# DeltaNet's 16 x 16 diagonal blocks: inverted by matrix products on TensorE, or by recursive doubling on VectorE behind a trip through DRAM

## Time and profile before

| | us |
|---|---|
| median of 3 runs | 1150.86 (1150.45 to 1152.09) |
| the profiled execution | 1150.29 |
| its span, as the profile shows it | 1148.4 |
| TensorE busy | 1133.1 |
| VectorE busy | 707.2 |
| ScalarE busy | 548.3 |
| GpSimd busy | 0.9 |

### The profile page before, as it was taken

One profiled execution on the slowest core, in us unless ns is written; L12 is line 12 of the kernel. 1 busy time (PEld: TensorE's weight loads), 2 busy tenths in 40 slices (PEclk: granted clock), 3 DMA queues, 4 the chain that ended last, 5 costly groups with the idle time before them and its releaser, 6 DMA issues.

```text
span 1148.4 us, 19809 instructions
## 1 busy us (share of the span) xinstructions
PE 1133.1 (99%) x8837; PEld 1099.6 (96%) x8837; DVE 707.2 (62%) x754; ACT 548.3 (48%) x626; POOL 0.9 (0%) x10
## 2 busy tenths in 40 slices
PE   8999999999999999999999999999999999999998
PEld 8999999989999899999999999999999899999986
DVE  5756644678785766655545756564558847756542
ACT  5544343455642765344434643444456746544541
POOL 0000000000000000000000000000000000000000
PEclk9999999999999999999999999999999999999999
DMA  9556457776532145554554555555553225556540
GB/s 314 170 184 200 154 168 167 142 168 128 99 114 74 37 148 184 184 179 154 173 179 160 181 164 170 175 170 170 184 170 111 74 85 165 189 187 203 166 165 37
DMA packets 170307, 179.21 MB, mean 156 GB/s; under 512 B 4944, under 2 KB 163168, under 8 KB 170224
## 3 DMA queue, kind: packets, MB, share of 16 engines
q1 hardware_dynamic: 170224, 177.96, 50.9%
HBM read 176.90 MB, written 1.05 MB: 155 GB/s over the span
## 4 chain that ended last, share of the span: by engine, by line
PE 91%; DVE 4%; ACT 3%; issue 1%; DMA 1%; SPq 0%; DVEq 0%; ACTq 0%
PE ps L1674 23%; PE ps L1676 23%; PE ps L1675 23%; PE ps L1778 8%; PE ps L1891 2%; PE ps L1763 2%; PE ps L1762 2%; PE ps L1761 2%; PE ps L1711 2%; PE ps L1712 1%; PE ps L1708 1%; DVE w_lo L1103 1%; PE ps L1745 1%; ACT w_hi L664 1%; ACT u_hi L721 1%
## 5 line engine op out<-in xcount | busy, mean ns | idle before, releaser
L1674 PE MATMUL ps<-u_hi,w_hi 128*128 128x272 f32 (+1 forms) x1656 | 480.3, 290 | 2.1 <-DVE w_lo L1103 1.4
L1676 PE MATMUL ps<-u_hi,w_lo 128*128 128x272 f32 (+1 forms) x1656 | 476.5, 288 | 0.0
L1675 PE MATMUL ps<-u_lo,w_hi 128*128 128x272 f32 (+1 forms) x1656 | 474.4, 286 | 0.0
L1103 DVE TENSOR_TENSOR w_lo<-raw,w_hi 128x2048 fp32r<-128x2048 f32 (+1 forms) x168 | 372.0, 2236 | 120.9 <-ACT w_hi L664 120.9
L664 ACT ACTIVATE w_hi<-raw 128x2048 fp32r<-128x2048 f32 (+1 forms) x168 | 312.5, 1869 | 165.3 <-PE ps L1676 144.0
L1674 PEld LDWEIGHTS ps<-u_hi,w_hi 128*128 128x128 f32 x1656 | 311.9, 188 | 4.7 <-DVE w_lo L1103 1.9
L1675 PEld LDWEIGHTS ps<-u_lo,w_hi 128*128 128x128 f32 x1656 | 311.9, 188 | 0.3
L1676 PEld LDWEIGHTS ps<-u_hi,w_lo 128*128 128x128 f32 x1656 | 311.9, 188 | 0.0
L1674 PE MATMUL ps<-hid_hi,w_hi 128*128 128x272 f32 x528 | 152.1, 288 | 0.0
L1676 PE MATMUL ps<-hid_hi,w_lo 128*128 128x272 f32 x528 | 151.9, 288 | 0.0
L1675 PE MATMUL ps<-hid_lo,w_hi 128*128 128x272 f32 x528 | 151.8, 287 | 0.0
(11 more groups left out here) (334 smaller groups left out, 1156.7 us busy)
## 6 DMA issues: line engine op xcount, KB each, us to landing
raw<-ffn_w_up SPq DMA_DIRECT2D x44, 1024.0 KB, 5.1
raw<-ffn_w_gate SPq DMA_DIRECT2D x43, 1024.0 KB, 5.1
raw<-ffn_w_down SPq DMA_DIRECT2D x24, 896.0 KB, 4.8
raw<-ffn_w_down SPq DMA_DIRECT2D x20, 1024.0 KB, 5.2
raw<-ab_w_in SPq DMA_DIRECT2D x16, 1024.0 KB, 13.8
raw<-cd_w_in SPq DMA_DIRECT2D x9, 1024.0 KB, 5.1
raw<-ab_w_out SPq DMA_DIRECT2D x4, 1024.0 KB, 4.9
raw<-cd_w_out SPq DMA_DIRECT2D x4, 1024.0 KB, 5.0
```

The costliest lines, as they stand in the source:

```text
L1103: dve.tensor_tensor(dst, src, w_hi[:, n % NW, 0:rows(n) * CB].bitcast(F32), ALU.subtract)\
L1674: pe.matmul(o, wh, rhs_hi[:, kk, tok], start=first and kk == 0, stop=False)
L1675: pe.matmul(o, wh, rhs_lo[:, kk, tok], start=False, stop=False)
L1676: ins = pe.matmul(o, wl, rhs_hi[:, kk, tok], start=False, stop=last and kk == rows(n) - 1)
```

```diff
# GpSimd, in mixer ab
+                    pool.wait_ge(s_A, 1)
+                    pool.dma_start(a_dram[0:P * 9 * P].rearrange("(p x) -> p x", p=P),
+                                   dN[:, :, :].rearrange("p q c -> p (q c)")).then_inc(s_stored, 16)
+                    pool.wait_ge(s_stored, 16)
+                    near = a_dram.rearrange("(b r) -> b r", b=8)[:, 0:BK * 9 * P]\
+                        .rearrange("b (i q c) -> q b i c", i=BK, q=9)[:, :, :, 0:BK]
+                    for q in range(9):
+                        pool.dma_start(blk_a[8 * q:8 * q + 8, 0:BK * BK].rearrange("b (i j) -> b i j", j=BK), near[q])\
+                            .then_inc(s_blk, 16)
+                    pool.wait_ge(s_inv, 1)
+                    pool.dma_start(i_dram.rearrange("(n x) -> n x", n=NBK), blk_i[:, 0:BK * BK]).then_inc(s_istored, 16)
+                    pool.wait_ge(s_istored, 16)
+                    pool.dma_start(blk_x[:, :, :], i_dram.rearrange("(q p j) -> p q j", p=P, j=BK)).then_inc(s_iload, 16)
# VectorE, the inverses of the blocks
+                def block_inverses():
...
+                    step.done(dve.tensor_scalar(blk_a[:, 0:BK * BK], blk_a[:, 0:BK * BK], -1.0, None, ALU.mult))
+                    step.done(dve.tensor_copy(blk_i[:, BK:BK * BK:2 * 17], blk_a[:, BK:BK * BK:2 * 17]))
+                    for s_ in (2, 4, 8):
...
+                        for left, right, res in ((low, first, y), (second, y, to)):
+                            if s_ == 2:
...
+                            t = blk_t[:, 0:n * s_ ** 3].rearrange("n (b r c m) -> n b r c m", b=n, r=s_, c=s_)
+                            for i in range(n):
+                                ins = dve.tensor_tensor(
+                                    t[:, i, :, :, :], left[:, i, :, :].unsqueeze(2).to_broadcast([NBK, s_, s_, s_]),
+                                    right[:, i, :, :].rearrange("n m c -> n c m").unsqueeze(1).to_broadcast([NBK, s_, s_, s_]),
+                                    ALU.mult)
+                            step.done(ins)
+                            for i in range(n):
+                                ins = dve.tensor_reduce(res[:, i, :, :], t[:, i, :, :, :], AX.X, ALU.add)
# VectorE, the order
                 evac(6)
                 lo(b + 8)
-                for g, (lo_, hi_) in enumerate(GROUPS):
...
                 conv(2)
                 evac(7)
+                dve.wait_ge(s_eye, 2)
+                dve.wait_ge(s_blk, 16 * 9)
+                block_inverses()
                 lo(b + 9)
-                doubled(1, 0)
                 conv(3)
-                doubled(1, 1)
-                doubled(1, 2)
                 lo(b + 10)
                 rotate(0)
                 dve.wait_ge(s_l2r, 2)
                 dve.tensor_tensor(gq[:, :, 0:T], gq[:, :, 0:T], l2r[:, :, :], ALU.mult).then_inc(s_l2, 1)
-                doubled(2, 0)
-                doubled(2, 1)
                 lo(b + 11)
-                doubled(3, 0)
...
+                dve.wait_ge(s_iload, 16)
+                for g in range(3):
+                    start_inverse(g)
+                dve.wait_ge(s_ATc, 3)
+                off_diagonal(0)
+                rotate(1)
+                lo(b + 12)
# TensorE, the order
                 proj(7, 1)
-                pe.wait_ge(s_P, POWERS.index((0, 1)) + 1)
-                doubling(1, 0)
-                pe.wait_ge(s_X0, 3)
-                doubling(0, 2)
                 pe.wait_ge(s_evac, 7)
                 proj(8, 0)
-                doubling(1, 1)
-                doubling(1, 2)
                 proj(8, 1)
                 pe.wait_ge(s_l2sq, 3)
+                pe.wait_ge(s_ATc, 3)
                 l2_sum(1)
                 pe.wait_ge(s_evac, 8)
                 proj(9, 0)
                 pe.wait_ge(s_l2r, 2)
-                doubling(2, 0)
-                doubling(2, 1)
...
+                pe.wait_ge(s_ktail, 1)
+                for g, (lo_, hi_) in enumerate(GROUPS):
+                    pe.wait_ge(s_X0, g + 1)
+                    for q in range(lo_, hi_):
+                        ins = pe.transpose(col(4 + g, q), XX[:, 0, q, :], ident[:, :])
+                    ins.then_inc(s_XT, 1)
+                proj(10, 1)
+                pe.wait_ge(s_XTc, 3)
+                merge_first(0)
```

More of the change, by code:

```diff
@@ L78 @@
 AB_EVAC = (0, 1, 2, 3, 4, 5, 6, 7, 12, 13, 14, 15)
-ROUNDS = ((0, 0), (0, 1), (1, 0), (0, 2), (1, 1), (1, 2), (2, 0), (2, 1), (3, 0), (3, 1), (2, 2), (3, 2))
-POWERS = [x for x in ROUNDS if x[0] < 3]
-DOUBLES = [x for x in ROUNDS if x[0] > 0]
+NBK, BK = 9 * 8, 16
+BKW = 17 * BK
+GAP = BK * 9 * P + BK
 AB_SPLITS = 3
@@ L108, in shape_constants @@
     masks[:, LOWER32] = (i > j) & (i // TAIL == j // TAIL)
-    masks[:, DIAG16] = -1.0 * (i // 16 == j // 16)
+    masks[:, DIAG16] = i // 16 == j // 16
     for n, size in enumerate((16, 32, 64)):
@@ L253, in build @@
         mix_lo = at("mix_lo", [P, HR, T], F32R, conv_place)
+        blk_x = sb("blk_x", [9, BK])
+        pp_place = r_place - 4 * 9 * P * 4
+        blk_a = at("blk_a", [NBK, BKW], F32, pp_place)
+        blk_t = at("blk_t", [NBK, 8 * 8 * 8], F32, pp_place + 4 * BKW)
+        blk_y = at("blk_y", [NBK, 64], F32, pp_place + 4 * (BKW + 512))
+        blk_i = at("blk_i", [NBK, BKW], F32, pp_place + 4 * 9 * P)
         assert place[0] <= nc.sbuf_usable_end
@@ L288, in build @@
         ps = ctx.enter_context(nc.psum_tensor("ps", [P, 8, BANK], F32))
+        a_dram = nc.dram_tensor("a_dram", [8 * GAP], F32).ap()
+        i_dram = nc.dram_tensor("i_dram", [NBK * BK * BK], F32).ap()
         s_in = sem("inputs_loaded")
@@ L386, in build @@
         s_ATc = sem("A_transposed_copied")
-        s_PP0 = sem("first_power_ready")
+        s_eye = sem("block_identity_set")
+        s_stored = sem("A_stored")
+        s_blk = sem("A_blocks_loaded")
+        s_inv = sem("block_inverses_ready")
+        s_istored = sem("block_inverses_stored")
+        s_iload = sem("block_inverses_loaded")
         s_gdec = sem("qk_inputs_decayed")
@@ L465, in blocks @@
             return ps[:, bank, 0:(hi_ - lo_) * P].rearrange("p (n c) -> p n c", c=P)
[L467 to L474, removed]
         def over(col, shape):
@@ L645, in _ @@
                     pool.memset(ba[:, :, :], 0.0).then_inc(s_pads, 1)
+                    pool.memset(blk_i[:, :], 0.0).then_inc(s_eye, 1)
+                    pool.wait_ge(s_eye, 1)
+                    pool.memset(blk_i[:, 0:BK * BK:BK + 1], 1.0).then_inc(s_eye, 1)
+                    pool.wait_ge(s_A, 1)
[11 more added lines that the diff above has]
+                    pool.dma_start(blk_x[:, :, :], i_dram.rearrange("(q p j) -> p q j", p=P, j=BK)).then_inc(s_iload, 16)
                 if kind == "cd":
@@ L784, in raw_copy @@
                     act.activation(chunk_of(n), two(AB_BANK[n]), ACT.Copy).then_inc(s_rraw, 1)
[L786 to L792, removed]
                 def merge_copy(m):
@@ L875, in ab @@
                 l2_square(gq, 0, 4)
-                powers(1, 1)
-                powers(1, 2)
                 act.preload_act_table_set(EXP_SET)
@@ L881, in ab @@
                 hi(b + 11)
-                powers(2, 0)
-                powers(2, 1)
                 raw_copy(1)
                 act.preload_act_table_set(SILU_SET)
-                powers(2, 2)
                 hi(b + 12)
-                for g, (lo_, hi_) in enumerate(GROUPS[:2]):
+                for g, (lo_, hi_) in enumerate(GROUPS):
                     act.wait_ge(s_XT, g + 1)
-                    act.activation(XX[:, 0, lo_:hi_, :], blocks(4 + g, lo_, hi_), ACT.Copy).then_inc(s_XTc, 1)
+                    act.activation(XX[:, 1, lo_:hi_, :], blocks(4 + g, lo_, hi_), ACT.Copy).then_inc(s_XTc, 1)
                 tap(4)
@@ L1231, in rotate, with part @@
                     dve.wait_ge(s_rot, i + 1)
-                def doubled(r, g):
-                    lo_, hi_ = GROUPS[g]
[L1236 to L1240, removed]
+                def block_inverses():
+                    def part(t, s_, off):
+                        return t[:, :].rearrange("n (b x) -> n b x", x=17 * 2 * s_)[:, :, off:off + 16 * s_]\
+                            .rearrange("n b (r x) -> n b r x", x=BK)[:, :, :, 0:s_]
+                    step.done(dve.tensor_scalar(blk_a[:, 0:BK * BK], blk_a[:, 0:BK * BK], -1.0, None, ALU.mult))
+                    step.done(dve.tensor_copy(blk_i[:, BK:BK * BK:2 * 17], blk_a[:, BK:BK * BK:2 * 17]))
+                    for s_ in (2, 4, 8):
+                        low, first, second, to = (part(blk_a, s_, 16 * s_), part(blk_i, s_, 0), part(blk_i, s_, 17 * s_),
+                                                  part(blk_i, s_, 16 * s_))
+                        n = 8 // s_
+                        y = blk_y[:, 0:n * s_ * s_].rearrange("n (b r c) -> n b r c", b=n, r=s_)
+                        for left, right, res in ((low, first, y), (second, y, to)):
+                            if s_ == 2:
```

(33 more changed lines are left out.)

23 lines of the change are left out of this document (removed).

## The result

The changed kernel takes 1154.32 us (median of 8 runs, 1151.84 to 1155.23), the kernel before 1150.65 (8 runs, 1150.37 to 1152.09). The ratio is 1.0029, 95% interval 1.0019 to 1.0039: slower by 0.3%, 3.3 us by the ratio and 3.7 by the two medians. The profiled execution took 1153.98 us, its span is 1152.1.

The account below looks back on a forecast made before the run. TensorE's issue time (busy 99%) bounds the kernel. A 17.9 us stall against 16.75 gained gives +1.2, plus 2.5 for the clock, +3.7: 1154.5 us from a 1150.86 median, said as 1154.3; 8-in-10 range 1146.0 to 1161.0.

Parts of the forecast that it names:

- What is taken away: TensorE's doublings: 72 products at 0.223 us and a 0.8 us wait go, one transpose comes; 16.75 us gained.
- Where the wait falls: TensorE before l2_sum(1): idle from 286.0 to 303.9, 17.9 us, behind transfers, inverses and VectorE's queued work.
- The store: First trip, A (576 KB) from SBUF to DRAM, slowed by chunk 12: 5.7 us (2.9 to 9).
- GpSimd's pitch: Time between GpSimd's issues of the nine block loads: 1.2 us, bounded by 0.45 and 1.9.
- The last landing: Ninth block load: 1.9 us to land plus 0.9 of slower issue beside chunk 13; blocks in at 290.75.
- rival 3: Small pieces crawl beside chunk 13, or second trip outruns its cover: +13 us, 1164; chance 0.12 for over +8 us.
- The number: Whole kernel: +1.2 us of net stall and 2.5 of clock, 1154.5 by the sum, 1154.3 said.
- The inverses: block_inverses() on VectorE, 20 results, after the blocks land: 6.1 us (5.5 to 7.5).
- The clock: TensorE restarts at 1.2 GHz after its idle stretch: 2.5 us lost (1.7 to 3.4).
- The second round trip: 72 KB store and 1152-piece load of the inverses: 15.1 us, hidden under 16 to 18 us, 3 to spare.
- Rival 1: Blocks back by 284.7, stall shorter than gain: faster by over 0.2%, likely -4 us, 1147; chance 0.20.
- rival 2: Stall about cancels gain, clock included, ninth load landing 284.7 to 289.4: 1148.6 to 1153.2 us; chance 0.25.

Follow-up runs that it names:

- The last run: Changed kernel with chunks 12 and 13 held on SP and VectorE's order made conv(3), inverses, low half of chunk 10, first rotation: 1136.99 us, ratio 0.9881.
- the run with 70 products: Changed kernel plus 70 useless TensorE products before its wait for the squares of q: 1153.43 us, ratio 1.0025.
- 79 products: Changed kernel plus 79 useless TensorE products before its wait for the squares of q, leaving no gap there: 1152.21 us, ratio 1.0015.

## Why the prediction was right, point by point

- **What is taken away.** 72 products of 0.223 us, the 0.8 us wait, one more transpose: 16.75 us. The last run has 14.1 us of gain and 1.5 us of new wait; 1.1 us remain between this and the sum, no more than the spread of that run's four times (1135.95 to 1137.51). The term stands.
- **Where the wait falls.** It fell before `l2_sum(1)`, by the chain that was read from the order: blocks, inverses, low half of chunk 9, `conv(3)`, silu, square. 17.4 us measured, 17.9 forecast, TensorE released at 303.50 against 303.9.
- **The terms inside it were less good than their sum.** A was ready 0.4 us later in this execution. The store took 4.0 us where 5.7 was taken (2.9 to 9). Its fixed part of 1.3 us came from no row, since the earlier trace rows have 1.9 us for 64 KB beside the 2.0 for 256, and the doubling by chunk 12 did not come. GpSimd's pitch was 0.60 us, half of the 1.2 and 1.3 taken between 0.45 and 1.9: nine issues took 5.4 us. The last landing took 8.35 us where 2.8 was taken. Together the loads had 13.2 us in the forecast and took 13.1 (276.72 to 289.84): two errors cancelled, by luck. The forecast put the cost into the issue and gave chunk 13 at most 0.9 us. The runs show 4.7 us that go with chunk 13 (8.35 against 3.69 with it held) and some 1.7 more with chunk 12 (3.69 against 2.0 with both held, where VectorE's order had changed too). This mechanism stood in rival 3, small pieces that share with the chunk and crawl, which had 0.12. All nine did take longer, 4.7 us or more in place of 2.0; but GpSimd's issues are cheap and the landings overlap, so its price of +8 us and more did not come.
- **The number.** The forecast's own sum is 1154.5; 1154.3 was said, without a reason for the difference, and 1154.32 was measured. A match that close is luck: behind it stand errors of +0.4 us (A), -1.7 (store), -5.6 (issues), +5.5 (last landing) and +0.6 (inverses). TensorE's waits before the change add up to 9.7 us and not to "some 8"; nothing hangs on it.
- **The inverses.** 6.7 us against 6.1. The sums of 512 took the 0.68 us of the earlier trace rows; the two products of 512 took 1.01 and 1.07 and not the 0.68 of the earlier trace rows, together 0.7 us more; all before them took 3.2 us, where 3.3 was taken.
- **The clock.** 2.5 us forecast, 1.6 to 2.7 measured. It fell at 288.7, 2.6 us after TensorE's last tile, and came back at 309.2, after 5.7 us of work at 1.2 GHz.
- **The second round trip.** Hidden, as forecast, and faster: the store landed in 1.9, the load of 1152 pieces in 3.2 us, where the 1152 pieces alone had 9.6. Taking a 64-byte piece to cost as much as a 1 KB piece of the weights was wrong by far. What the loss of that cover costs was shown by the run with the inverse later: the same store took 8.5 us beside a chunk, and 10.9 us of wait came up.
- **Rival 1** would by its own formula have been right, at -3.6 us, if the ninth load had landed 2 us after its issue, at 283.5. Two chunks stood between. Holding chunk 13 alone brought the landing to 284.8 and gave -4.0 us: no change from the kernel before, which is rival 2. With chunk 12 held as well, in this order of VectorE, nothing was run.
- The Trainium skill, DMA: Bandwidth & Descriptors, section Anatomy of one DMA — SWDGE (gpsimd) path, has 2.0 us plus bytes over 436e3 for a transfer issued by GpSimd. Where no weights were in flight the traces agree for 8 KB (2.0 us) and for the 72 KB store in two runs (1.9), not in the third (2.9). The 72 KB load in pieces of 64 bytes took 3.1 to 3.6 us, where the estimate by the fit is 2.2. The 576 KB store took 3.7 and 4.2 with chunk 12 held, where that estimate is 3.4.
- The Trainium skill, DMA: Bandwidth & Descriptors, section Queues, rings and completion order, says that an engine takes turns between its queues packet by packet. One could read this as a small delay, a share of the small transfer's own size. That reading fails here: the 72 KB store took 8.5 us beside a chunk and 1.9 without. No run here shows in which order an engine took its packets, so whether the page's sentence itself holds stays open.

## What to carry to other kernels

Work that is moved off the busiest engine onto a trip through DRAM costs what is queued behind its wait, not what it takes itself: the same trip and the same inverses made this kernel 3.3 us slower and, with nothing needed behind the wait and the big loads held out of the way, 14.1 us faster. Before a short transfer that something waits for, look which large transfer will be in flight at that moment, in the new schedule and not in the old one; a prefetch that has slack can be held by one wait. And a sum that comes out right says little of its terms: the chain of the changed kernel showed that the issue was cheap, and the run with chunk 13 held that the neighbour was dear.

## What the runs showed of the hardware

- Small transfers of GpSimd's queue took several times longer with a 1 MB weight chunk in flight: 8 KB loads 4.7 us or more in the changed kernel against 1.9 to 2.1 with both chunks held, the 72 KB store 4.3 to 8.5 us against 1.9 to 2.9. In the three cases above the last one landed 0.1 to 0.3 us behind a chunk (289.84 against 289.7, 305.7 against 305.4, 294.8 against 294.6); others landed well before one. The chunks beside them took 8.9 to 11.4 us (12.8 for one issued 1 us behind another), the same chunks of the kernel before, with no small transfer, 8.5 to 10.2. Why it is so was not taken apart: the size of the chunk's pieces, the spacing of its rows in DRAM and the order within the DMA engines were not varied.
- GpSimd issues a load of 128 pieces in 0.60 us, SP in 0.31 to 1.20 us for the same load; the nine took 5.36 and 5.96 us.
- 1152 pieces of 64 bytes landed in 3.1 to 3.6 us in one transfer, while 1024 pieces of 1 KB of this weight matrix took 8.5 or more.
- An elementwise product of 512 elements with both operands repeated over strides took 1.01 to 1.18 us on VectorE, a plain one 0.68.
- In the run with 70 products the clock fell at 305.7, shortly before the end of a gap of 2.4 us, and TensorE worked at 1.2 GHz until 309.1; with the gap filled by 79 products it stayed at 1.00. After the 1.5 us before the squares of q, in the three runs that had it, it stayed at 1.00 too, until the wait at the transposes in two of them. Whether the length of the gap alone makes the difference was not tried.
